# First feed-forward of the second block in one pass over 512 rows, with its weights split in place

## What is computed

```
x = x + gt2 * squared_relu_mlp(modulate_2(rms_norm(x, norm2_g[i]), sh2, sc2), mlp_w1[i], mlp_w2[i])
if not last:
    ctx = ctx + mods_c[5] * squared_relu_mlp(modulate_2(rms_norm(ctx, norm2_g[i]), mods_c[3], mods_c[4]),
                                             mlp_w1[i], mlp_w2[i])
```

## Time and profile before

| | |
|---|---|
| Time, median of 3 runs | 2890.04 us (2889.53 to 2892.01) |
| Profiled execution: its span (the page gives no other time of it) | 2890.3 us |
| PE busy | 2770.7 us, 96% |
| PE weight loads busy | 1973.5 us, 68% |
| DVE busy | 1186.3 us, 41% |
| ACT busy | 709.9 us, 25% |
| Mean granted clock of PE | 0.976 of full speed |
| Chain that ended last, share on PE | 86% |
| Read from HBM | 682.52 MB |

### The profile page before, as it was taken

How to read it: one execution, slowest core, us unless ns; L and a number is a source line. 1 busy time by engine, 2 the same in 40 slices (tenths; PEclk the granted TensorE clock), 3 DMA queues, 4 the chain that set the end, 5 groups by cost and what they waited for, 6 DMA issues and landing times.

```text
span 2890.3 us, 49935 instructions
## 1 busy us (share of the span) xinstructions
PE 2770.7 (96%) x22276; PEld 1973.5 (68%) x22276; DVE 1186.3 (41%) x2055; ACT 709.9 (25%) x1136; POOL 48.3 (2%) x39
## 2 busy tenths in 40 slices
PE   8899999999999999999998999999999999998998
PEld 6788997877533333333332756899999965697998
DVE  4667764332301101101101587356555433553554
ACT  2234333131200000000000214334444322211443
POOL 0000000000000000000000000000000000131000
PEclk9899999999999999999999999999999998999999
DMA  8756765544899999999999225265554330010452
GB/s 334 304 182 260 277 259 204 190 175 150 347 373 421 421 420 421 420 421 420 421 412 421 74 97 193 73 262 204 190 182 160 140 117 15 24 54 24 181 184 80
DMA packets 95198, 686.88 MB, mean 238 GB/s; under 512 B 10624, under 2 KB 11776, under 8 KB 11904
## 3 DMA queue, kind: packets, MB, share of 16 engines
q1 hardware_dynamic: 94400, 681.37, 60.5%
q10 hardware_dynamic: 576, 2.25, 0.2%
HBM read 682.52 MB, written 1.05 MB: 237 GB/s over the span
## 4 chain that ended last, share of the span: by engine, by line
PE 86%; DMA 6%; DVE 5%; ACT 2%; issue 1%; SPq 0%; POOL 0%; ACTq 0%; DVEq 0%
PE ps L530 42%; PE ps L2053 15%; PE ps L890 12%; PE ps L801 6%; PE ps L2078 5%; DMA AR<-W 3%; DMA ring<-W 2%; PE ps L543 2%; PE ps L2081 2%; PE ps L776 1%; PE ps L2061 1%; DVE macc L646 0%; DMA XT<-XIN 0%; SPq L3577 0%; ACT AR L1761 0%
## 5 line engine op out<-in xcount | busy, mean ns | idle before, releaser
L2053 PE MATMUL ps<-AR 128*32 128x512 f32 x2904 | 440.1, 593 | 11.6 <-DMA AR<-W 10.2
L530 PE MATMUL ps<-HT,ring 128*128 128x256 f32 (+1 forms) x1696 | 443.4, 422 | 1.7 <-ACT HT L719 1.7
L530 PEld LDWEIGHTS ps<-HT,ring 128*128 128x128 f32 x1696 | 324.2, 193 | 114.5 <-issue 75.0
L530 PE MATMUL ps<-FR,FR 128*128 128x256 f32 x3120 | 387.4, 284 | 0.0
L530 PEld LDWEIGHTS ps<-FR,FR 128*128 128x128 f32 x3120 | 378.7, 192 | 3.0 <-issue 2.9
L872 DVE TENSOR_TENSOR FR<-ring,FR 128x2048 fp32r<-128x2048 f32 x129 | 294.4, 2291 | 164.4 <-ACT FR L856 164.4
L890 PE MATMUL ps<-FR,FR 128*128 128x256 f32 x2832 | 349.0, 283 | 0.0
L890 PEld LDWEIGHTS ps<-FR,FR 128*128 128x128 f32 x2832 | 343.8, 192 | 0.0
L2173 DVE TENSOR_TENSOR AR<-AR,ps 128x256 f32<-128x256 f32 x70 | 29.6, 423 | 678.9 <-ACT AR L2136 361.0
L2053 PE MATMUL ps<-ring,AR 128*32 128x512 f32 x1576 | 288.8, 594 | 5.8 <-DMA ring<-W 3.5
L856 ACT ACTIVATE FR<-ring 128x2048 fp32r<-128x2048 f32 x129 | 244.7, 1908 | 130.9 <-PE ps L890 85.2
(11 more groups left out here) (430 smaller groups left out, 2517.1 us busy)
## 6 DMA issues: line engine op xcount, KB each, us to landing
ring<-W SPq DMA_DIRECT2D x431, 1024.0 KB, 5.8
AR<-W SPq DMA_DIRECT2D x215, 1024.0 KB, 21.0
XT<-XIN ACTq DMA_DIRECT2D x2, 1024.0 KB, 8.7
cst<-CS SPq DMA_DIRECT2D x1, 1859.0 KB, 14.3
out<-XT SPq DMA_DIRECT2D x4, 256.0 KB, 2.2
sml<-SM SPq DMA_DIRECT2D x1, 970.5 KB, 10.3
cst<-CS ACTq DMA_DIRECT2D x1, 129.5 KB, 8.1
sml<-SM ACTq DMA_DIRECT2D x1, 16.0 KB, 5.7
```

The source lines that it names most:

```text
L530: ins = g.matmul(out, l, r, **kw)
L2053: ins = g.matmul(bank.ap[group(i), :], mo.hg[e % 2][:, 4 * h + k, group(t)], w[n][:, k, :], start=j == 0 and k == 0, stop=j == 1 and k == ...
```

## The change

`m0` becomes one pass over all 512 columns, in three functions of its own (`wide_pe`, `wide_act`, `wide_dve`); `m1` keeps the old code, with the parameter q taken out. The 32 slots are loaded and split once (`SLOTS` falls from 646 to 614).

- PE: up slots 0 and 1 for the latent half (256 columns), then the sums of the context half's norm, one background step, up slots 0 and 1 for the context half, then up slots 2 to 15 with 512 columns into two banks each, with a background step after 3 to 10. Then 16 down slots with 512 columns, adding into all eight banks. The last slot runs bank by bank. Then the sums for the next stage's norm.
- The low part of a slot is written over the slot in the ring (`ring_low` is the ring seen as float32r), so the place is given back only when PE has used the slot. High parts have two places (`wide_w`): slot i is split after slot i - 2 has been used. The input's low part lies over `HT` (`HT_low`), its high part in `wide_x`; the whole hidden layer is kept (`wide_h`, 32 x 512), and its low part is written over it. High parts of hidden pairs go round five places of `wide_x`; the first is free from the start, the other four hold the input's high part until up slot 15 is done.
- Ring places are given out by the order in which the slots of this stage are used (`given_back`), not by slot number.
- The norm of the next stage's latent half comes after the pass.

```
-def early_step(block, c, r):
-
-    return 1 if block == 0 and c == 0 and r < 23 - ATTENTION_STEPS else 0
+def wide_steps(n):
+
+    return 1 if n == 1 or 3 <= n < 25 - ATTENTION_STEPS else 0
...
+    load("m0_1", 2)
+    for n in range(16):
+        if n == 1:
+            bg.go(wide_steps(n))
+        load("m0_1" if n < 14 else "m0_2")
+        if n != 1:
+            bg.go(wide_steps(n))
+    load("m0_2", 14)
+    bg.finish("ada1")
...
-                where.append(places.take(range(RING), i, i))
+                where.append(places.take(range(RING), i, given_back.get(i, i)))
...
+        class InPlace(Splits):
...
+            def pair(self, i):
+                return self.hi[:, i % 2, :], ring_low[:, where[slot(*self.names[i])][0], :]
...
+                    g.tensor_tensor(low, src, high.bitcast(F32), SUB).then_inc(*s.done(self.x + ".lo", i))
...
+            latent, context = slice(0, 256), slice(256, 512)
+            up(0, latent, 0)
+            down_end("ev.down1")
+            up(1, latent)
+            norm_pe(g, s, "m0", (1,))
+            bg.go(wide_steps(1))
+            for n in range(2):
+                up(n, context, 1 if n == 0 else None).then_inc(*used(n))
+            for n in range(2, 16):
+                up(n, slice(0, 512)).then_inc(*used(n))
+                bg.go(wide_steps(n))
+            acc = [counts.take("m0.down", m, keep=True) for m in range(8)]
+            for i in range(15):
+                s.wait_ge("m0.lo", 16 + i).wait_ge("m0.d_lo", i)
...
+            s.wait_ge("m0.lo", 31).wait_ge("m0.d_lo", 15)
+            for m in range(8):
+                for kk in range(2):
+                    ins = down(15, kk, m)
...
+            s.mark("m0.end")
+            norm_pe(g, s, "odd")
...
+            for n in range(16):
+                s.wait_ge("m0.used", n)
+                for h in range(2):
+                    g.activation(wi.H[:, 2 * n + h, :], counts.bank("m0.up", n, h)[:, :], ACT.Relu).then_inc(
+                        *s.done("m0.relu", n, h, empties=("m0.up", n, h)))
+                w.make_act(g, s, n + 3)
+                if n == 8:
+                    hidden(0)
+            hidden(1)
+            hidden(2)
+            for i in range(16):
+                w.make_act(g, s, min(16 + i + 3, 32))
+                if i + 3 < 16:
+                    hidden(i + 3)
+            s.mark("m0.end")
+            squares_act(g, s, "odd", odd_ready(s), 0)
+            norm_root_act(g, s, "odd", 0)
+            shift_act(g, s, "odd", MN["ada1"][0], 0)
...
+            residual_dve(g, s, "ev.down1", ("down", "ev.down1", 3), M, 16, 1)
+            bg.go(wide_steps(1))
+            norm_dve(g, s, "m0", HT, mod_weight("ada0", 1), pair, M, 24, (1,))
...
+            for m in range(8):
+                s.wait_ge("m0.bank", m)
+                ps = counts.bank("m0.down", m)
+                for c in range(2):
+                    g.scalar_tensor_tensor(out=XT[:, c, m, :], in0=ps[:, c * 256:c * 256 + 256], scalar=M[:, 40 + m, c:c + 1], in1=XT[:, c, m, :], op0=MUL,
+                                           op1=ADD).then_inc(*s.done("res", f"m0.down{c}", m, empties=("m0.down", m) if c else None))
+            s.mark("m0.end")
+            norm_dve(g, s, "odd", HT, mod_weight("ada1", 0))
```

More of the change, by code:

```diff
@@ L2614, in mlp_pairs @@
[L2614 to L2619 removed]
+        wi = Stage()
+        with ExitStack() as first:
+            wi.fr = first.enter_context(nc.sbuf_tensor("wide_w", [128, 2 * SLOT], F32R))
+            wi.xd = first.enter_context(nc.sbuf_tensor("wide_x", [128, 5 * 1024], F32R))
+            wi.H = first.enter_context(nc.sbuf_tensor("wide_h", [128, 32, 512], F32))
@@ new lines, in mlp_act @@
+        def mlp_act(g, s):
+            w = Splits("m1", ml.names, ml.fr, PARTS, from_ring)
+            w.make_act(g, s, 3)
+            norm_act(g, s, "m1", lambda h, k: s.wait_ge("res", "od.down", k))
+            shift_act(g, s, "m1", MN["ada1"][0], 24, ml.pairs[0])
+            for n in range(17):
+                if n < 16:
+                    w.act(g, s, 2)
+                    s.wait_ge("m1.used", ml.at["m1_1", n])
+                    if n >= 2:
+                        s.wait_ge("m1.d_lo", n - 2)
+                    g.activation(ml.hid[n % 2], pair2(counts.bank("m1.up", n)), ACT.Relu).then_inc(*s.done("m1.relu", n, empties=("m1.up", n)))
+                    s.wait_ge("m1.hid", n)
+                    if n >= 3:
+                        s.wait_ge("m1.used", ml.at["m1_2", n - 3])
+                    g.activation(ml.d[0][:, n % 3, :, :], ml.hid[n % 2], ACT.Copy).then_inc(*s.done("m1.d_hi", n))
+                if n:
+                    w.act(g, s, 2)
+            s.mark("m1.end")
```

333 lines of the change are left out of this document (185 added, 148 removed).

## The result

| | before | after |
|---|---|---|
| Time, median of 8 runs each (us) | 2889.39 (2885.41 to 2892.01) | 2899.65 (2893.29 to 2901.57) |
| Ratio, 95% interval | | 1.0031 [1.0021, 1.0041] |
| Span of the profiled execution | 2890.3 | 2899.6 |
| First matmul of `m0` to first `HT,ring` matmul | 389.07 | 395.64 (forecast 368.2) |
| First matmul of `m0` to first `AR,sml` matmul | 413.44 | 422.73 |

A forecast was written before the change was run, and what follows sets the result against it. PE, busy for 96% of the span, was taken as the bound. 23.0 + 312.5 + 13.8 + 6.9 + 0.6 + 5.7 + 7.3 = 369.8 for 389.1, 19.3 us less: 2871 us, range 2864 to 2880.

The forecast's parts named there:

- (f): End of `m0`: PE waits for the next stage's latent-half norm, 5.7 us idle plus 1.6 of slow clock, 7.3.
- (a): Up slots 0 and 1 of `m0` stay in halves: 192 matmuls of 256 columns at 0.120, 23.0 us.
- (b): 14 up and 16 down slots of `m0`: 1440 matmuls of 512 columns at 0.217, 312.5 us.
- (c): Background steps in `m0`'s up slots stay nine, after slots 1 and 3 to 10: 13.8 us.
- (d): The two norms' sums stay on PE, 6.9 us, and the small matmul ahead of `od_in` takes 0.6.
- (e): After the first background step PE waits for the context half's scaling: 4.1 us idle plus 1.56 of slow clock, 5.7.
- (g): Across `m0`, halved splits and loads bring nothing under PE and no supply is late; 0 to 0.3 us at slot 2.
- second rival: In `m0`, 256 columns bound by 0.107 plus a fixed 0.013, so 512 take 0.2263: 13.4 us more, 2884 us; 6%.
- Columns are not free: In `m0`, a 512-column float32r matmul is worked as two of 256, 2 x 0.120: 2904 us, slower; 4%.
- The weights were never late: Rival: in `m0`'s up slots, weight loads take 12 us and seven steps wait 1.6 each: 2882 us; 4%.
- 0.131 a matmul: Rival: `m0`'s 512-column matmuls overlap their streams at about 131 ns each, 124 us more off, to 2747; 1%.

The follow-up runs named there:

- e_all2: Changed kernel with two PSUM banks passed over behind up slot 10 and both norms' context-half work reordered: 2876.71 us, 0.9957 of the kernel before.
- lab runs: Changed kernel plus measuring groups of matmuls into an unread PSUM bank, behind the last down slot or early up slots; 64 columns took 0.111 us; no whole-kernel time given.
- first lab run: Changed kernel plus groups of 48 matmuls of 64 to 512 columns behind the last down slot; 512 columns took 0.2267 us each; no whole-kernel time given.

## Why the prediction was wrong

To the first `HT,ring` matmul my terms give 368.2, since 1.6 of the 7.3 in (f) stand behind that mark; 395.64 was measured, 27.4 more. The measured terms are sums over the profiled records of the stretch; what the half clock cost is the difference to the same matmuls in the version without waits (e_all2), where the clock stays up.

| term | forecast | measured | difference |
|---|---|---|---|
| (a) 192 matmuls of 256 columns | 23.0 | 0.1177 each: 22.6 | -0.4 |
| (b) 1440 of 512 columns | 312.5 | 0.2311 each: 332.8 | +20.3 |
| starts of groups in (a) and (b) | 0 | 1.4 | +1.4 |
| (c) background steps | 13.8 | 11.8 | -2.0 |
| (d) sums and small matmul | 7.5 | 7.5 | 0.0 |
| (e) wait at the context half's norm | 4.1 + 1.6 | 4.0 + 2.2 | +0.5 |
| (f) wait at the next stage's norm, idle | 5.7 | 5.7 | 0.0 |
| (g) wait at slot 11 | 0 | 5.4 + 2.2 | +7.6 |
| sum | 368.2 | 395.6 | +27.4 |

Behind the mark the fall of the clock took 2.7 instead of 1.6 (27.09 us to `AR,sml` instead of 24.37). 2870.7 + 27.4 + 1.1 = 2899.2, against 2899.65 measured.

**(b) is the step that failed**, with two parts of different kinds. I took 0.119 from the one-column rows as the price of a weight load, called the 0.120 of 256 columns "that same price", and gave 512 columns the gap of plain matmuls. The 0.119 was a wrong reading of my own rows: it is the mean of 15 distances, and the first of them, behind the last `HT,ring` matmul, is 0.22 (2326.30 to 2326.52). From the second load on, the trace of the kernel before shows

```profile
2326.52 1.75 PEld L530 LDWEIGHTS ps<-cst,AR 128*128 128x128 f32 x15
```

that is (1.75 - 0.19) / 14 = 0.111, and the records of 64 columns in the lab runs stand 0.111 apart as well. So the load wasn't the bound at 256; columns plus 0.0133 was. That is the second rival, a fixed gap, with 6%. Its price for (b), 325.9 at 0.2263, is 13.4 of the 20.3 (at the 0.2267 measured it is 13.9). Read rightly, the rows of before already left 0.009 of the 0.120 that no load explains; what spoke against the rival, the 0.003 of plain matmuls, came from another data type. The Trainium skill (TensorE: Matmul & The Clock Gate, "LDWEIGHTS (loading the stationary operand)") gives 107 ns for the load; 0.111 with 64 columns is nearer to it than my 0.119, and I had set that figure aside on the strength of the misread rows.

The other 6.4 of (b) are the ring's place, which no row of before shows: there the ring never was an operand of a float32r matmul. Moving the ring took back 5.65 in the whole stretch, with the cause left open above. The low part "written over the slot in the ring" was costed for the place that it keeps, not for where PE reads it.

**(g) "Nothing is late" failed too, at one instruction.** I had followed the banks only from up to down, and the copy `mrow<-ps` only at step 1. The last step hands its sums to another instruction, the copy to `M_ada`, which DVE does behind a split. In both kernels the bank of the sums is the second to be handed out after the last step. A round of the kernel before took one, so its next user, up slot 10, began at 2010.5, a round after the copy (at 1999.2, right behind the sums). A wide slot takes two, so the very next one waits for the bank. For the rest (g) was right: no wait for a weight, 6.2 us as median of the loads, no wait at slots 2 and 3 and none between up and down.

**What held:** (e) and (f), each wait in its place, its releaser and its idle time to 0.2 us; and that nothing changes outside of the stretch. The clock behind the waits was sized too small, by 0.6 and 1.1. (c) was too dear by 2.0: the nine steps take their own records' 11.8 and nothing beside them (the 1.53 a step came from one pair of rounds).

**The rivals.** "Columns are not free" landed nearest in time, and its threshold of 0.2304 a matmul was crossed (0.2311), yet its mechanism isn't the one: a 512-column matmul is not worked as two. The weights were never late, and 0.131 a matmul wasn't seen anywhere. The range was too narrow because its top (2880) took in no rival at all, although "a fixed gap" rested on the same row as my own value.

## What to carry to other kernels

A mean over distances hides an odd one: look at the single distances before a price is taken from them. A price at one size doesn't tell a fixed part from a part that grows: before 1440 matmuls rest on a reading of 0.120, look for, or measure, the same operation at a second size. When slots get wider, follow every PSUM bank to the instruction that empties it, background work included, and see what stands ahead of that instruction on its engine; here one bank cost 7.6 us. Waits of 4.0 to 5.7 us cost 2.2 to 2.7 us of half clock on top of their idle time; those of 1.6 and 0.4 in the version without the three waits cost none. And a transfer or a norm that used to hide behind a second pass can be hidden again by order alone: the same one-pass plan with its waits taken out and the ring moved is 0.53% faster than the kernel before, where as first written it was 0.31% slower.

## What the runs showed of the hardware that I had not expected

- At full clock a float32r matmul took one cycle of 2.4 GHz a column plus 0.0133 us (0.120, 0.1733, 0.2267 for 256, 384, 512), a plain float32 record two cycles a column plus 0.003 (0.216 for 256). A single weight tile loaded again and again cost the same.
- An operand of the ring at bytes 16512 to 57472 of a partition, as weights or as columns, made it 0.2333 with 512 columns, 0.1733 with 384 (no change) and 0.117 with 256 (less). With the ring at 73120 it was 0.2267 and 0.120, though `HT_low` then lay at 56736. A shift by 32 bytes changed no sum. Whether it is the place or the start counted to 512 bytes is open.
- The granted clock fell while PE stood busy throughout. In the first lab run it was 1.00 from 2265 to 2269, in the group of 64 columns; the 48 records of 128 columns behind it took 10.28 / 48 = 0.214, at a granted clock of 0.50, the 1.2 GHz level, and within the group of 256 columns that follows it was back at 1.00. The row of the 128-column group:

```profile
2271.00:2279.00 8.00, 8.00 (x40) 8.00 (x39) 0.00 (x0) 0.00 (x0) 0.00 (x0) 0.50 0.00 0
```
